# Sums of squares by single-pass products of ones with a high and a low part

## What is computed

```python
def l2norm(x):
    return x * lax.rsqrt(jnp.sum(x * x, axis=-1, keepdims=True) + EPS)
...
    q = jnp.repeat(l2norm(q.reshape(Bn, T, N_QK_HEADS, HEAD_K)), rep, axis=2)
...
    o, S = gated_delta_rule(q, k, v, g, beta, s_gdn.astype(jnp.float32))
    o = rmsnorm(o, gdn_norm) * jax.nn.silu(z.reshape(Bn, T, N_V_HEADS, HEAD_V).astype(jnp.float32))
```

## Time and profile before

| what | value |
| --- | --- |
| median of 3 runs | 2613.81 us (2609.17 to 2616.22) |
| span of the profiled execution | 2610.9 us; its own time beside the span isn't listed |
| PE busy | 2551.5 us (98%) |
| DVE, ACT, POOL busy | 1662.5 (64%), 1320.8 (51%), 529.4 us (20%) |
| mean granted clock of PE | 0.99 of full speed |
| the eight groups | until about 1015 us |

### The profile page before, as it was taken

One profiled execution on the slowest core, in us unless ns is written; L12 is line 12 of the kernel. 1 busy time (PEld: TensorE's weight loads), 2 busy tenths in 40 slices (PEclk: granted clock), 3 DMA queues, 4 the chain that ended last, 5 costly groups with the idle time before them and its releaser, 6 DMA issues.

```text
span 2610.9 us, 50479 instructions
## 1 busy us (share of the span) xinstructions
PE 2551.5 (98%) x20848; PEld 2529.6 (97%) x20848; DVE 1662.5 (64%) x2861; ACT 1320.8 (51%) x2013; POOL 529.4 (20%) x913
## 2 busy tenths in 40 slices
PE   7999999999999999999999999999999999999997
PEld 7999999999999999999999999999999999999997
DVE  6757777685857675533365566466776656776665
ACT  6545546464645544433344344455665545665663
POOL 1527162543627160000000000100100000110100
PEclk8999999999999999999999999999999999999998
DMA  7646455555646456677755556757986667985563
GB/s 213 181 129 194 135 168 147 165 159 159 174 130 195 133 168 178 196 207 202 208 173 179 184 188 207 246 179 240 315 283 220 217 187 250 316 282 189 164 207 108
DMA packets 445718, 507.38 MB, mean 194 GB/s; under 512 B 21329, under 2 KB 423914, under 8 KB 443066
## 3 DMA queue, kind: packets, MB, share of 16 engines
q1 hardware_dynamic: 417072, 415.43, 52.1%
q0 software_dynamic: 27840, 88.53, 11.2%
q10 hardware_dynamic: 578, 0.19, 0.0%
HBM read 478.16 MB, written 26.49 MB: 193 GB/s over the span
## 4 chain that ended last, share of the span: by engine, by line
PE 61%; POOL 1%; DMA 1%; DVE 1%; issue 0%; ACT 0%; DVEq 0%; POOLq 0%; ACTq 0%
PE bank L702 60%; DMA raw<-in_w_ffn_down 1%; POOL sol L554 1%; POOL prod L551 1%; DVE wlo L1330 0%; ACT whi L1005 0%; PE bank L726 0%; DMA raw<-in_w_ple_gate 0%; DVE xlo L1370 0%; DMA sol_scratch<-sol 0%; DVEq L228 0%; DMA DT<-sol_scratch 0%; POOL sol_scratch L584 0%; POOL DT L588 0%; ACT pp L1196 0%
## 5 line engine op out<-in xcount | busy, mean ns | idle before, releaser
L702 PE MATMUL bank<-xhi,whi 128*128 128x264 f32 x5520 | 1593.0, 289 | 6.0 <-DVE wlo L1330 3.0
L702 PE MATMUL bank<-xlo,whi 128*128 128x264 f32 x5520 | 1569.0, 284 | 0.0
L702 PE MATMUL bank<-xhi,wlo 128*128 128x264 f32 x5520 | 1566.9, 284 | 0.0
L1330 DVE TENSOR_TENSOR wlo<-raw,whi 128x1024 fp32r<-128x1024 f32 x828 | 1013.8, 1232 | 730.5 <-ACT whi L1005 729.9
L1005 ACT ACTIVATE whi<-raw 128x1024 fp32r<-128x1024 f32 x828 | 873.9, 1058 | 780.5 <-PE bank L702 710.2
L702 PEld LDWEIGHTS bank<-xhi,whi 128*128 128x128 f32 x5520 | 1042.7, 189 | 9.0 <-issue 5.3
L702 PEld LDWEIGHTS bank<-xlo,whi 128*128 128x128 f32 x5520 | 1043.2, 189 | 2.0 <-issue 1.9
L702 PEld LDWEIGHTS bank<-xhi,wlo 128*128 128x128 f32 x5520 | 1039.8, 188 | 0.0
L702 PE MATMUL bank<-ahi,whi 128*128 128x264 f32 x704 | 200.1, 284 | 2.2 <-DVE wlo L1330 2.2
L702 PE MATMUL bank<-ahi,wlo 128*128 128x264 f32 x704 | 200.1, 284 | 0.0
L702 PE MATMUL bank<-alo,whi 128*128 128x264 f32 x704 | 199.7, 284 | 0.0
(11 more groups left out here) (300 smaller groups left out, 1839.8 us busy)
## 6 DMA issues: line engine op xcount, KB each, us to landing
raw<-in_w_in SPq DMA_DIRECT2D x356, 512.0 KB, 4.1
raw<-in_w_ffn_gate SPq DMA_DIRECT2D x88, 512.0 KB, 5.2
raw<-in_w_ffn_up SPq DMA_DIRECT2D x88, 512.0 KB, 4.7
raw<-in_w_ffn_down SPq DMA_DIRECT2D x96, 384.0 KB, 3.1
raw<-in_w_gdn_out SPq DMA_DIRECT2D x64, 512.0 KB, 3.4
chunkS<-in_state_gdn POOLq DMA_DIRECT2D x16, 1024.0 KB, 7.4
raw<-in_w_sconv_out SPq DMA_DIRECT2D x32, 512.0 KB, 3.4
raw<-in_w_o SPq DMA_DIRECT2D x32, 512.0 KB, 4.1
```

The costliest lines, as they stand in the source:

```text
L702: return pe.matmul(out, lhsT, rhs, start=start, stop=stop)
L1330: dve.tensor_tensor(wlo[:, at_ % SPLIT, :, :], raw[:, at_ % RAW, :, :], f32(whi[:, at_ % SPLIT, :, :]), ALU.subtract).then_inc(lo_ready, 1)
```

## The change

Two sums of squares are made from a rounded part and a rest. ACT makes each square twice, once rounded to float32r (`sq_hi`) and once in full. DVE subtracts the two (`q_lo`, `o_lo`, both float32r, in place of the full squares). PE multiplies ones in float32r by the high part and by the low part into the same accumulator. So each full product becomes two single-pass ones, three ACT instructions of 512 columns and two DVE instructions (512 and 1024 columns) are added in each group, and PE's two steps wait for a DVE step. `sq_hi` takes the place of `cs`.

```diff
-    ones = new("ones", [P, P])
+    ones_r = new("ones_r", [P, P], F32R)
+    ones = ones_r[:, :].bitcast(F32)
...
+    sq_hi = at("sq_hi", [P, NCH, 4 * CH], F32R, sv_at)
+    o_lo = at("o_lo", [P, NCH, 4 * CH], F32R, pt_at)
+    q_lo = at("q_lo", [P, NCH, 4 * CH], F32R, qk_at)
...
-        DVE_STEP = {"cur": {0: ("exponents",), 5: ("lt",), 13: ("qn",), 16: ("qkt",), 26: ("mask",), 27: ("e0",),
+        DVE_STEP = {"cur": {0: ("exponents",), 5: ("lt",), 10: ("qlo",), 13: ("qn",), 16: ("qkt",), 26: ("mask",), 27: ("e0",),
                             28: ("ktok",), 29: ("u0",), 31: ("r",)},
-                    "prev": {1: ("e1",), 3: ("u1",), 4: ("s2",), 9: ("o",)},
+                    "prev": {1: ("e1",), 3: ("u1",), 4: ("s2",), 6: ("olo",), 9: ("o",)},
...
                 elif slot == "qsum":
-                    pe.wait_ge(g["qsq"], gr + 1)
+                    pe.wait_ge(g["qsq"], 2 * gr + 2)
                     if gr > 0:
                         pe.wait_ge(g["olog"], gr)
-                    mm(B[4][:, :], ones[:, :], QK[:, 1, :]).then_inc(g["qsum"], 1)
+                    mm(B[4][:, :], ones_r[:, :], sq_hi[:, 0, :], True, False)
+                    mm(B[4][:, :], ones_r[:, :], q_lo[:, 1, :], False, True).then_inc(g["qsum"], 1)
...
                 elif slot == "osum":
-                    pe.wait_ge(g["osq"], gr + 1)
+                    pe.wait_ge(g["osq"], 2 * gr + 2)
                     pe.wait_ge(g["s2"], gr + 1)
-                    mm(B[4][:, :], ones[:, :], PT[:, 0, :])
-                    mm(B[7][:, :], ones[:, :], PT[:, 1, :]).then_inc(g["osum"], 1)
+                    for c in range(NCH):
+                        mm(B[4 + 3 * c][:, :], ones_r[:, :], sq_hi[:, c, :], True, False)
+                        m = mm(B[4 + 3 * c][:, :], ones_r[:, :], o_lo[:, c, :], False, True)
+                    m.then_inc(g["osum"], 1)
...
                 if slot == "qsq":
                     act.wait_ge(silu_done, 4 * gr + 2)
+                    act.activation(sq_hi[:, 0, :].rearrange("p (b t) -> p b t", b=2), sqk[:, 0:2, 0:T], ACT.Square)
...
                     act.activation(vTok[:, 0, :, :].rearrange("p b c -> p (b c)"), bank[6][:, :], ACT.Copy)
+                    act.activation(sq_hi[:, 0, :], bank[6][:, :], ACT.Square)
                     act.activation(PT[:, 0, :], bank[6][:, :], ACT.Square)
...
+                    act.activation(sq_hi[:, 1, :], bank[7][:, :], ACT.Square)
                     act.activation(PT[:, 1, :], bank[7][:, :], ACT.Square).then_inc(g["osq"], 1)
...
+                elif slot == "qlo":
+                    dve.wait_ge(g["qsq"], 2 * gr + 1)
+                    dve.tensor_tensor(q_lo[:, 1, :], QK[:, 1, :], f32(sq_hi[:, 0, :]), ALU.subtract).then_inc(g["qsq"], 1)
+                elif slot == "olo":
+                    dve.wait_ge(g["osq"], 2 * gr + 1)
+                    dve.tensor_tensor(o_lo[:, :, :], PT[:, :, :], f32(sq_hi[:, :, :]), ALU.subtract).then_inc(g["osq"], 1)
```

More of the change, by code:

```diff
@@ L153, in trunk @@
     Tt = new("Tt", [P, NCH, 4 * CH])
+    qk_at = top[0]
     QK = new("QK", [P, NCH, 4 * CH])
     Nn = new("Nn", [P, NCH, 4 * CH])
+    pt_at = top[0]
     PT = new("PT", [P, NCH, 4 * CH])
@@ L494, in _ @@
             mine.inc(pool.memset(ident[:, :], 0.0))
-            mine.inc(pool.memset(ones[:, :], 1.0))
+            mine.inc(pool.memset(ones_r[:, :].bitcast(F32), 1.0))
             mine.inc(pool.memset(eps[:, :], EPS))
```

## The result

The changed kernel took 2628.66 us (median of 6 runs, 2626.20 to 2630.91), the one before beside it 2611.62 (6 runs, 2606.99 to 2616.22): +17.0 us, a ratio of 1.0065 with a 95% interval of 1.0054 to 1.0077. The forecast was +15.6, that is 2629.4, in a range of 2619 to 2642.

What follows compares the result with a forecast made beforehand. PE, 98% busy, bounds the kernel except before pt, where it waits for DT. 7 x 4.9 = 34.3 us, minus 15.8 and 3.3, plus 0.1 (last group) and 0.3 (POOL), gives +15.6, or 2629.4 us; range 2619 to 2642.

Steps and rivals of the forecast that it cites:

- The bound and the give-back: Between kk and pt the chain to DT bounds, not PE; 15.8 us of waits and 3.3 of clock losses vanish.
- The saving: osum and qsum: two single-pass products of 0.235 us replace one of 0.86, saving 0.39 a sum, 9.4 us over 24 sums.
- The wait at osum: PE at osum waits 3.71 us for olo behind DVE's queue in 7 groups, 0.85 in the last group.
- The clock: After the 3.71 us wait PE's clock falls to its lower level, losing 2.3 us a group, bounds 0 and 2.88.
- The second wait: PE at qsum waits for qlo: hardly at all with the clock loss, 1.8 us without it.
- the prediction's own sign: The forecast would be wrong if a group came out longer by other than 2.2 us on average.
- POOL: qlo and olo hold POOL up at most 1.85 us a group on the chain to DT, hidden while PE is late.
- my third rival: PE is held by POOL, not by olo: +13.0 us minus 0.8, so 2626 us; chance 0.05.
- Not slower: Only the first wait stays, net 2.6 us a group, and DT waits and clock losses offset it: 2613 us; chance 0.10.
- The DT wait is no bound: The wait for DT isn't really a bound and all 9.4 us saved reach the end: 2604.4 us; chance 0.03.
- The single-pass products cost as much as full ones: Ones products with high and low parts cost two times 0.43 us: +8.2 us on the forecast, 2638; chance 0.06.
- A longer clock loss: The clock falls for longer and again at a second wait: 7.1 us a group, +31 us, 2644; chance 0.12.

Runs made afterwards that it cites:

- e9: The kernel before, with the last 6 of 31 steps of POOL's solve left out; 25.8 us faster than before.
- e5: The kernel before, with each full sum made twice on PE; 2614.5 us against 2611.0.
- e4: e3 with "o" also moved behind q_lo (j = 9 to j = 11); 4.4 us slower than the kernel before.
- e3: The changed kernel with o_lo moved to j = 5, before lt on DVE; 6.9 us faster than the kernel before.
- e12: e7 with the last 6 of 31 steps of POOL's solve left out; 11.4 us below e11.
- e11: The changed kernel with "o" moved behind q_lo and the last 6 of 31 steps of POOL's solve left out; 36.5 us above e9.
- e2: The changed kernel with the queries' part taken back, outputs' part kept; +18.5 us by medians against the kernel before.
- e7: The changed kernel with "o" moved behind q_lo and 28 products added on PE ahead of its o_lo wait; 4.2 us slower by medians than without these products.
- e1: The changed kernel with the outputs' part taken back, queries' part kept; 4.8 us faster than the kernel before.

## Why the prediction was right

**The bound and the give-back: right.** The earlier trace rows were read as slack on PE's side, 15.8 us in seven groups and 3.3 of clock. e9 shows 25.8 us for all of it with the first group (20.2 + 2.9 + 3.3 = 26.4 by the prediction's rows), e5 that PE's work there is nearly free. After the change the seven waits are gone.

**The saving: right.** 0.23 us between starts against 0.235 (behind a wait the first distance is 0.34, so osum took 1.04 us in place of 0.94 even at the upper clock). Had it been 0.216, 48 products would have taken 0.9 us less, not the 1.7 that the prediction has. In the changed kernel, where PE's own path decides, the saving comes off PE's lateness; where PE is given no new wait, as in e4, it goes into the wait for DT and ends nowhere but in the last group.

**The wait at osum: right.** From kk to osum PE takes 7.96 us against 4.23, that is 3.73 more, forecast 3.71. Its cause, DVE's queue and not DVE's load, is shown by e3, which moves one instruction and loses the wait. In the last group it was 0.71 against 0.85.

**The clock: right in kind and nearly in size.** Five stretches of 3.4 us and two of 6.8, at half speed, are 15.3 us lost at most, 2.2 a group against 2.3. That an idle stretch is what costs it is shown by e12 against e11. How many microseconds a single wait loses isn't told by its length: seven waits of 3.55 to 3.58 us had stretches of 6.8, of 3.4 and, once, of none.

**The second wait: mis-sized.** It was forecast as 0 with a clock loss and 1.8 without. It came to 0.27 to 1.97 us, 0.95 on average, also in groups with a clock loss: in four of these six the products of osum ran at half speed (0.43 between starts in place of 0.23), partly in a fifth, so ACT's roots and all of DVE behind them came 0.8 later, where I had allowed 0.5, and q_lo took 0.72 in place of 0.62. With it PE's lateness at pt is 73.64 - 67.95 = 5.7 us against 4.9. On the sum that is 7 x 0.8 = +5.6, of which a first group 1.5 shorter than forecast and a give-back of 7 x (70.38 - 67.95) + 3.7 = 20.7 in place of 19.1 take away 3.1: the total came nearer than its terms, which is luck. By the prediction's own sign, a group longer by other than 2.2 us, this term shows: a group came out (22.8 - 3.7) / 7 = 2.7 us longer.

**POOL: right that it is hidden, too low in size.** The bound was 1.85 us later on the chain to DT. It came 66.60 - 64.38 = 2.2 later, and not by the way named: o_lo runs before the solve begins (431.50 against 444.08), and without q_lo, in e2, the solve takes the same 38.8. A part (0.7) lies before the solve, where POOL first waits for the stores of rows that ACT stages behind "oroot", so behind osum; a part (1.1) is in the solve, 38.8 against 37.7, and the rest behind it. PE's 5.7 covers it with about 1 us to spare (66.6 + 6.0 from issue to pt, as before the change, is 72.6, against 73.6). e7 shows the other side: as soon as PE is quicker, POOL's path is the bound. A kernel held by POOL, my third rival, was therefore close behind the forecast, though by another way, and a change that only freed PE could gain about 1 us a group at most.

**The rivals.** Not slower: out, the lateness is 5.7 against a deciding 2.7. The DT wait is no bound: out by e5. The single-pass products cost as much as full ones: out by the timeline. A longer clock loss: seen in two groups of seven, not in all.

## What to carry to other kernels

Before one takes work from the busiest engine, one should look in which stretch it lies and what that stretch waits for at its end: here PE was busy 98% of the time, and all but a twelfth of the saved products lay before a wait on another chain. When a step starts to depend on an engine with a queue, the cost is the place in that queue; moving one instruction (e3) turned +17 us into -6.9. And two paths of nearly one length have to be told apart by shortening one, since removing a wait on the other (e7) shows nothing.

## What the runs showed of the hardware

POOL's elimination, the same 62 operations each time, took from 36.2 to 40.4 us in the seven like groups, and longer where more of DVE's splits ran during it. In one group each of e3, before, after and e7, in this order, the count and mean duration of the splits within the solve:

```profile
L1342 DVE TENSOR_TENSOR wlo<-raw,whi 128x1024 fp32r<-128x1024 f32 x12 | 15.2, 1283 | 2.4 <-ACT whi L1014 2.4
```

```profile
L1330 DVE TENSOR_TENSOR wlo<-raw,whi 128x1024 fp32r<-128x1024 f32 x13 | 16.3, 1284 | 3.9 <-ACT whi L1005 3.9
```

```profile
L1342 DVE TENSOR_TENSOR wlo<-raw,whi 128x1024 fp32r<-128x1024 f32 x14 | 17.6, 1284 | 2.9 <-ACT whi L1014 2.9
```

```profile
L1345 DVE TENSOR_TENSOR wlo<-raw,whi 128x1024 fp32r<-128x1024 f32 x15 | 18.8, 1284 | 3.2 <-ACT whi L1017 3.2
```

The solves around them took 36.2, 37.1, 38.9 and 40.3 us. In these four one split more goes with 0.9 to 1.8 us more, 1.4 on average. A longer solve also sees more splits by itself (13 in 37.1 us are one every 2.9), so the count is partly a result and not only a cause. A stall of PE inside the solve goes with a shorter one, since DVE then splits less: in e1, where PE waits 1.8 to 1.9 us for q_lo, it took 36.9 on average, and in e4, without that wait, 38.4. That the splits cause this was read from the traces of the ten kernels with the whole solve, and not tested by removing them. The rule of the Trainium skill (SBUF — State Buffer, SBUF: two separate sides), that a DVE operation with two SBUF inputs and a GpSimd operation that reads SBUF shut each other out for a whole instruction, would give this. The 1.16 us of one POOL step beside two splits, against 0.36 just before them, agree with it.
